# The delta rule's doubling levels with 64 moving columns instead of 128, stale columns cleared by GpSimd, the loop over levels unrolled

## The reference

```python
def chunked_gated_delta_rule(q, k, v, g, beta):
    G = jnp.cumsum(g, axis=-1)
    decay = jnp.where(lower_incl, jnp.exp(jnp.where(lower_incl, diff, 0.0)), 0.0)
    m = jnp.where(strict, jnp.einsum('bhncd,bhnsd->bhncs', kb, k) * decay, 0.0)
    a_mat = eye + m
    t_mat = lax.linalg.triangular_solve(a_mat, eye, left_side=True, lower=True)
    u = jnp.einsum('bhncs,bhnse->bhnce', t_mat, vb)
    w = jnp.einsum('bhncs,bhnsd->bhncd', t_mat, kb * jnp.exp(G)[..., None])
    attn = jnp.einsum('bhncd,bhnsd->bhncs', q, k) * decay
    # then, chunk by chunk:
    v_new = u_n - w_n @ state
    o_n = qg_n @ state + attn_n @ v_new
    state = state * exp(gl_n) + k_dec.T @ v_new
```

## Time and profile before

| | us |
|---|---|
| median of 3 executions | 2548.59 (2548.0 to 2549.6) |
| the profiled execution, its own time | 2549.39 |
| its span, first to last instruction | 2547.5 |
| its mean granted clock | 0.939 |

### The profile page before, as it was taken

The page is one execution under the profiler, slowest core; times in us unless marked ns, Lnnn a source line. Parts: engine busy times, 40 slices in busy tenths (PEclk is TensorE's granted clock), DMA queues, the critical chain, the costliest instruction groups (busy, mean ns, idle before and its releaser), DMA issues.

```text
span 2547.5 us, 32468 instructions
## 1 busy us (share of the span) xinstructions
PE 2315.7 (91%) x11904; PEld 1958.9 (77%) x11904; DVE 1683.0 (66%) x2158; ACT 1157.6 (45%) x1664; POOL 354.2 (14%) x141
## 2 busy tenths in 40 slices
PE   8998998899989989989989899899797847999999
PEld 6887887778868878878887688688687836887877
DVE  5765665478667757756654687677566643667997
ACT  4444453364444434444533644444352013546875
POOL 3531000000025315410000000244001010000000
PEclk9998999889989989999988899899899956999999
DMA  8765543234657657656432345576340000657996
GB/s 299 237 211 150 166 133 104 88 124 136 195 184 237 214 164 237 226 153 175 132 109 86 113 145 181 174 238 225 108 140 10 0 1 6 208 189 252 358 361 235
DMA packets 320162, 426.91 MB, mean 168 GB/s; under 512 B 28192, under 2 KB 220080, under 8 KB 319904
## 3 DMA queue, kind: packets, MB, share of 16 engines
q1 hardware_dynamic: 315904, 412.45, 50.7%
q0 software_dynamic: 4016, 12.73, 1.7%
q10 hardware_dynamic: 112, 0.04, 0.0%
HBM read 424.06 MB, written 1.05 MB: 167 GB/s over the span
## 4 chain that ended last, share of the span: by engine, by line
PE 74%; DVE 8%; issue 8%; ACT 6%; DVEq 2%; DMA 1%; POOL 1%; PEld 1%; POOLq 0%; SPq 0%; ACTq 0%; PEldq 0%
PE ps L264 17%; PE ps L266 17%; PE ps L265 17%; PE ps L511 10%; PE ps L3167 4%; ACT hi L247 3%; DVE lo L251 2%; PE ps L297 2%; PE ps L1053 1%; ACT room L929 1%; DVE room L1138 1%; PE ps L502 1%; DMA raw<-in_w_up 1%; DVEq L1095 1%; DVEq L730 1%
## 5 line engine op out<-in xcount | busy, mean ns | idle before, releaser
L251 DVE TENSOR_TENSOR lo<-raw,hi 128x1024 fp32r<-128x1024 f32 x737 | 1012.6, 1389 | 618.3 <-ACT hi L247 612.2
L247 ACT CAST hi<-raw 128x1024 fp32r<-128x1024 f32 x737 | 769.1, 1048 | 867.9 <-PE ps L266 695.9
L264 PE MATMUL ps<-hi,xT_hi 128*128 128x512 f32 (+2 forms) x1440 | 575.9, 400 | 5.7 <-issue 5.0
L266 PE MATMUL ps<-hi,xT_lo 128*128 128x512 f32 (+2 forms) x1440 | 563.2, 391 | 0.0
L265 PE MATMUL ps<-lo,xT_hi 128*128 128x512 f32 (+2 forms) x1440 | 563.1, 391 | 0.0
L264 PEld LDWEIGHTS ps<-hi,xT_hi 128*128 128x128 f32 x1440 | 280.5, 195 | 58.7 <-issue 6.5
L266 PEld LDWEIGHTS ps<-hi,xT_lo 128*128 128x128 f32 x1440 | 279.7, 194 | 57.2
L265 PEld LDWEIGHTS ps<-lo,xT_hi 128*128 128x128 f32 x1440 | 280.6, 195 | 51.4
L681 POOL TENSOR_SCALAR room<-room,vecs 128x1536 f32<-128x1536 f32 x28 | 134.9, 4819 | 235.8 <-DMA room<-in_w_ada 235.8
L264 PE MATMUL ps<-xT_hi,hi 128*128 128x256 f32 x544 | 160.9, 296 | 0.0
L265 PE MATMUL ps<-xT_lo,hi 128*128 128x256 f32 x544 | 155.4, 286 | 0.0
(11 more groups left out here) (526 smaller groups left out, 3348.6 us busy)
## 6 DMA issues: line engine op xcount, KB each, us to landing
raw<-in_w_mix_in SPq DMA_DIRECT2D x368, 256.0 KB, 2.9
raw<-in_ffn_w_in SPq DMA_DIRECT2D x352, 256.0 KB, 3.4
raw<-in_ffn_w_out SPq DMA_DIRECT2D x176, 256.0 KB, 2.9
raw<-in_w_gate SPq DMA_DIRECT2D x128, 256.0 KB, 5.1
raw<-in_w_up SPq DMA_DIRECT2D x128, 256.0 KB, 6.6
raw<-in_w_down SPq DMA_DIRECT2D x128, 256.0 KB, 5.7
room<-in_w_ada SPq DMA_DIRECT2D x32, 768.0 KB, 6.4
raw<-in_w_branch SPq DMA_DIRECT2D x96, 256.0 KB, 3.0
```

Source lines behind the costliest of these rows:

```text
L247: nc.scalar.copy(hi[c.hi_slot][:, 0:c.cols], raw[c.slot][:, 0:c.cols]).then_inc(rounded, 1)
L251: nc.vector.tensor_tensor(lo[c.slot][:, 0:c.cols], raw[c.slot][:, 0:c.cols], hi[c.hi_slot][:, 0:c.cols], ALU.subtract).then_inc(split, 1)
L264: pe.matmul(out, a[0], b[0], start=start, stop=False)
L266: return pe.matmul(out, a[1], b[0], start=False, stop=stop)
```

## The change

Level v changes only every second block of 2^v columns of `T` and of `Tt`, 64 of 128 columns. The changed kernel multiplies only these. For `T` TensorE multiplies `mT` itself, not masked, with the even blocks of `T`, and VectorE masks the 64 resulting columns as it takes them out of PSUM into the even blocks of `U`. Then `Tt` times the even blocks of `U` changes `T`, and `U` times the odd blocks of `Tt` changes `Tt`. `U` as a whole is the stationary operand of the second, so its odd blocks, which hold values of earlier levels, are set to zero by GpSimd between levels. GpSimd also fills `T` and `Tt` with the identity and `U` with zero at the start. The triangle goes into the subtraction by a table of 0 and -1e30. ScalarE has no part in the levels. The loops are unrolled, the tail's semaphores are merged, and `carry(pe)` is dropped.

```diff
+        ("upto_least", np.where(p <= j, 0, NEG)),
-        parts.append((f"level{b}", ((j // b) % 2 == 1) & (p // b == j // b - 1)))
+        parts.append((f"level{b}", p // b == c // b * 2 + 1))
...
+        U_BANK, T_BANK, TT_BANK = (2, 4), (3, 5), (0, 6)
...
+        def blocks(self, ap, v, odd):
+            return ap.rearrange("p (n two b) -> p n two b", two=2, b=1 << v)[:, :, odd, :]
+        def of_slot(self, ap, s):
+            return ap[:, s * P:(s + 1) * P]
+        def product(self, bank, v):
+            return ps[:, bank, :].rearrange("p (n b) -> p n b", b=1 << v)
...
+            for e in range(2):
+                nc.gpsimd.tensor_copy(self.T[e].rearrange("p (s n) -> p s n", n=P), eye)
+            pool.wait_ge(self.split, self.SPLIT_QG)
+            for e in range(2):
+                nc.gpsimd.memset(self.U[e], 0.0)
+            for e in range(2):
+                ins = nc.gpsimd.tensor_copy(self.Tt[e].rearrange("p (s n) -> p s n", n=P), eye)
+            ins.then_inc(self.cleared, 1)
+            for v in range(LEVELS - 1):
+                for e in range(2):
+                    if v == 0:
+                        pool.wait_ge(self.level, e + 1)
+                    pool.wait_ge(self.upd_t, 2 * v + e + 1)
+                    nc.gpsimd.memset(self.blocks(self.U[e], v + 1, 1), 0.0).then_inc(self.cleared, 1)
...
-            carry(pe)
...
+            for v in range(LEVELS):
+                for e in range(2):
+                    if v == 0:
+                        pe.wait_ge(self.mats, self.MT + e + 1)
+                    else:
+                        pe.wait_ge(self.level, 2 * (v - 1) + e + 1)
+                    for s in range(8):
+                        t = self.of_slot(self.T[e], s) if v else ident
+                        ins = pe.matmul(ps[:, self.U_BANK[e], s * HD2:(s + 1) * HD2], self.mT[e][:, s, :], self.blocks(t, v, 0), start=True, stop=True)
+                    ins.then_inc(self.lt, 1)
                 for e in range(2):
...
+                    pe.wait_ge(self.masked, 2 * v + e + 1)
+                    if v:
+                        pe.wait_ge(self.level_t, 2 * (v - 1) + e + 1)
+                    else:
+                        pe.wait_ge(self.mats, self.AT + e + 1)
+                    if 0 < v < LEVELS - 1:
+                        for s in range(8):
+                            ins = pe.matmul(ps[:, self.T_BANK[e], s * HD2:(s + 1) * HD2], self.of_slot(self.Tt[e], s), self.blocks(self.of_slot(self.U[e], s), v, 0),
+                                            start=True, stop=True)
+                        ins.then_inc(self.upd, 1)
+                    if v:
+                        pe.wait_ge(self.cleared, self.START + 2 * (v - 1) + e + 1)
+                    for s in range(8):
+                        t = self.of_slot(self.Tt[e], s) if v else ident
+                        ins = pe.matmul(ps[:, self.TT_BANK[e], s * HD2:(s + 1) * HD2], self.of_slot(self.U[e], s), self.blocks(t, v, 1), start=True, stop=True)
+                    ins.then_inc(self.upd_t, 1)
...
-                    nc.scalar.copy(self.LT[e][:, 0:4, :], view_bank(4 * e, 4, P)).then_inc(self.lt0_done, 1)
...
-                V.tensor_tensor(self.e[e], self.e[e], bc(const("upto").unsqueeze(1), [P, 8, P]), ALU.mult)
+                V.tensor_tensor(self.mT[e], self.e[e], big(self.KK_BANK[e]), ALU.mult).then_inc(self.mats, 1)
+            for v in range(LEVELS):
+                at, b = CONSTS[f"level{1 << v}"][0], 1 << v
+                mask = consts[:, at:at + P // 2].rearrange("p (n b) -> p n b", b=b)
+                if v == 0:
+                    dve.wait_ge(self.cleared, self.START)
+                for e in range(2):
+                    dve.wait_ge(self.lt, 2 * v + e + 1)
+                    u = self.U[e].rearrange("p (s n two b) -> p s n two b", s=8, two=2, b=b)[:, :, :, 0, :]
+                    V.tensor_tensor(u, ps[:, self.U_BANK[e], :].rearrange("p (s n b) -> p s n b", s=8, b=b),
+                                    bc(mask.unsqueeze(1), [P, 8, P // 2 // b, b]), ALU.mult).then_inc(self.masked, 1)
+                    if v == 0:
+                        dve.drain()
+                        t = self.blocks(self.T[e], 0, 0)
+                        V.tensor_tensor(t, t, self.blocks(self.U[e], 0, 0), ALU.subtract).then_inc(self.level, 1)
+                if v == 0:
+                    dve.wait_ge(self.gram, self.QK)
+                    for e in range(2):
+                        V.tensor_tensor(self.aT[e], self.e[e], big(self.QK_BANK[e]), ALU.mult).then_inc(self.mats, 1)
+                for e in range(2):
+                    if 0 < v < LEVELS - 1:
+                        dve.wait_ge(self.upd, 2 * (v - 1) + e + 1)
+                        t = self.blocks(self.T[e], v, 0)
+                        V.tensor_tensor(t, t, self.product(self.T_BANK[e], v), ALU.subtract).then_inc(self.level, 1)
+                    dve.wait_ge(self.upd_t, 2 * v + e + 1)
+                    t = self.blocks(self.Tt[e], v, 1)
+                    V.tensor_tensor(t, t, self.product(self.TT_BANK[e], v), ALU.subtract).then_inc(self.level_t, 1)
                 dve.drain()
```

More of the change, by code:

```diff
@@ L2103, in build @@
         SPREAD0, SPREAD1, KK, QK = 1, 2, 3, 4
[L2104 to L2108, removed]
+        SPREAD_BANK, KK_BANK, QK_BANK = (0, 6), (2, 4), (0, 6)
+        level, level_t, upd, upd_t = sem("g_level"), sem("g_level_t"), sem("g_upd"), sem("g_upd_t")
+        mats, lt, masked, cleared = sem("g_mats"), sem("g_lt"), sem("g_masked"), sem("g_cleared")
+        MT, AT, START = 0, 2, 1
+        U_BANK, T_BANK, TT_BANK = (2, 4), (3, 5), (0, 6)
+        tail, tail_done, wT_done = sem("g_tail"), sem("g_tail_done"), sem("g_wT_done")
+        U0, STATE, VNEW, OUT = 1, 3, 5, 7
         raw = room[0:CT * CONV, 14000:14000 + P]
@@ L2119, in build @@
         e, mT, aT = ([view(room, 6144 + 2048 * n + 1024 * e, 8, P) for e in range(2)] for n in range(3))
[L2120 to L2123, removed]
+        U = [room[:, 12288 + 1024 * e:12288 + 1024 * (e + 1)] for e in range(2)]
+        T = [merged[:, e, :] for e in range(2)]
+        Tt = [xT_work[:, D * e:D * (e + 1)] for e in range(2)]
         vn = [view(hi_ring, 3072 + 512 * e, 8, HD2) for e in range(2)]
@@ L2213, in pe @@
             self.pe_gram(pe, self.QK_BANK, self.qT)
-            heads = self.heads
-            carry(pe)
[L2217 to L2229, removed]
@@ L2248, in pe @@
             cols = lambda h: slice(h * HD2, (h + 1) * HD2)
             for e in range(2):
-                pe.wait_ge(self.level, LEVELS * 2 + e + 1)
+                pe.wait_ge(self.level_t, 2 * (LEVELS - 1) + e + 1)
                 for h in range(4):
-                    pe.matmul(ps[:, 4 * e, cols(h)], self.Tt[e][:, h, :], self.head(self.vb, 0, e, h), start=True, stop=True)
-                    ins = pe.matmul(ps[:, 4 * e + 1, h * P:(h + 1) * P], self.both(self.kg, 1, h), self.Tt[e][:, 4 + h, :], start=True, stop=True)
@@ L2254, in pe @@
-                ins.then_inc(self.u0, 1)
+                    pe.matmul(ps[:, 4 * e, cols(h)], self.of_slot(self.Tt[e], h), self.head(self.vb, 0, e, h), start=True, stop=True)
+                    ins = pe.matmul(ps[:, 4 * e + 1, h * P:(h + 1) * P], self.both(self.kg, 1, h), self.of_slot(self.Tt[e], 4 + h), start=True, stop=True)
+                ins.then_inc(self.tail, 1)
             for e in range(2):
-                pe.wait_ge(self.u0_done, e + 1)
+                pe.wait_ge(self.tail_done, self.U0 + e)
@@ L2439, in dve @@
-            for e in range(2):
-                dve.wait_ge(self.lt, LEVELS * 2 + e - 1)
-                copy_lt(e)
-            for e in range(2):
-                dve.wait_ge(self.upd, LEVELS * 2 + e - 3)
-                V.tensor_tensor(self.Tt[e], self.Tt[e], big(4 * e), ALU.subtract)
-                dve.drain()
-                dve.sem_inc(self.level, 1)
-            for e in range(2):
-                dve.wait_ge(self.u0, e + 1)
-                V.tensor_copy(self.vn[e][:, 0:4, :], ps[:, 4 * e, 0:256].rearrange("p (h n) -> p h n", n=HD2)).then_inc(self.u0_done, 1)
```

81 lines of the change are left out of this document (19 added, 62 removed).

## The result

The changed kernel takes 2599.75 us (median, 2595.71 to 2600.88) against 2548.64 before: 1.0197 times, with an interval of 1.018 to 1.0215. The forecast was 2597. Its profiled execution took 2600.43 us, with a span of 2598.7 and a mean granted clock of 0.916 (0.939 before).

The account below looks back on a forecast made before the run. The level was taken as bound by its matmul count, with a short VectorE chain between. With the clock lost in level 0, +42.8 us to the tail and slower tail matmuls made +48.8, so 2597 us, range 2585 to 2609.

Parts of the forecast that it names:

- The bound and the price: Delta-rule levels: bound by matmul count; a 64-column matmul costs what 128 does, 0.223 us at 2.4 GHz, 0.427 at 1.2.
- The fall of the clock: Level 0, after its first products: TensorE waits 2.7 us for aT, the clock falls and stays down through all levels.
- 64-column matmuls neither hold nor win back 2.4 GHz.: Read from the delta rule's trace, 2032 to 2036 and 2108 to 2118 us: narrow matmuls stay at clock 0.50.
- Rival (A): Level 0's pause: the clock holds through the 2.7 us, matmuls cost 0.223 us, kernel takes 2533 us; chance 7%.
- Rival (B): Levels: the clock falls and comes back as TensorE runs without a gap, kernel takes 2536 us; chance 3%.
- The sum: Whole kernel: +42.8 us up to the tail's start and slower tail matmuls, in all +48.8, giving 2597 us.
- the +0.3: Start of the delta rule: subtractions as scalar_tensor_tensor cost 0 to 1.2 us more, taken as +0.3.
- The term for GpSimd beside VectorE: Angle computations after 1931 us: GpSimd's clearing beside them may cost 0 to 2 us; taken as 0, +2 kept.
- +6.0: The tail: its first 7 us run at 1.2 instead of 2.4 GHz, adding 3.3, 1.5 and 1.2 us.
- No wait on `g_cleared`: Levels: GpSimd's memset has over 10 us before TensorE's wait for it, so it costs nothing.
- (C): Levels: columns set the matmul price, half the columns cost half, kernel takes 2509 us; chance 1%.
- (D): First two levels: gapped columns or operand switches make 64 matmuls cost 0.617 instead of 0.427 us, 2609 us; chance 5%.

Follow-up runs that it names:

- experiment 6: Changed kernel, level 0's second product written to free banks so it need not wait, GpSimd's clearing moved behind the first subtractions: 2527.43 us; with clearing unmoved 2537.64 us.
- Experiment 8: Kernel without level 0's pause, clearing moved, with a short pause before level 3: one added clearing 2567.65 us, two 2568.40; one with 128 moving columns 2533.71.
- experiment 3: Changed kernel with 14 added unused matmuls of 128 moving columns filling level 0's pause: 2541.09 us.
- experiment 4: Changed kernel with 14 added unused matmuls of 64 moving columns filling level 0's pause: 2541.57 us, one of nine executions 2602.63.
- experiment 2: Changed kernel with only the first product of each level streaming its 64 moving columns twice, as 128: 2544.54 us.
- experiment 7: Kernel without level 0's pause, clearing moved, six added clearings making TensorE pause before level 3: 2576.69 us; with 128 columns and level 0's pause kept: 2542.33.
- experiment 5: Changed kernel with GpSimd's clearing of U and filling of Tt moved behind VectorE's first subtractions: 2597.26 us.
- experiment 1: Changed kernel with the levels' matmuls streaming their 64 moving columns twice, as 128: 2539.09 us.

## Why the prediction was right, point by point

**The bound and the price.** Right. The level is bound by the number of matmuls, and 64 columns cost what 128 do. At 1.2 GHz a level takes 20.48 us, 48 x 0.427. At 2.4 GHz it takes (2000.29 - 1946.70) / 5 = 10.72 in experiment 6, 48 x 0.223. That the weight loads of 128 columns set this price is argued from PEld, busy 96.00 of 96 us; no run changed the stationary columns.

**The fall of the clock.** Right in place and in consequence, with one part of the reasoning off. I put the pause (2.7 forecast, 2.79 measured) between one of 1.68 us that did no harm and one of 3.80 that did, as if its length decided. Experiment 8 shows that length is not the measure among 64-column matmuls: 1.37 us are enough. What I had put beside it, the 64-column work, is what decides: the run that differs only in having 128 columns kept its clock through the same 1.37 us. Whether the columns ahead of the pause or those behind it count was not separated.

**"64-column matmuls neither hold nor win back 2.4 GHz."** Half of that was wrong. They hold it, for 64 to 68 us in the kernels of experiments 3, 4 and 6. The rows I read it from, 2032 to 2036, are of the tail, where small pauses and matmuls over 64 rows are mixed in. The forecast rested on the other half, and that is true of the gap-free streams inside the levels, not everywhere: behind the QK gram (128 columns, at 1.2 GHz for 3.79 us) the clock came back 1.1 to 1.4 us into 64-column matmuls, in the changed kernel and in the same place in experiments 4 and 6 (there in the run with the clearing unmoved). In experiment 3, where it had fallen only inside the gram, it did not. What decides between these was not tested. Had the clock come back in the same way behind the pause of level 0, the forecast would have failed; it did in none of the executions of the changed kernel (2595.71 to 2600.88). Rival (A) is what happens as soon as the pause is gone: I gave it 2533, and the kernel without the pause, with the clearing where the change has it, takes 2537.64.

**Rival (B)**, that gap-free work brings the clock back, was cited from the Trainium skill, "TensorE: Matmul & The Clock Gate", section "Why this matters for your kernels". The runs bear it out for 128 columns (experiments 2, 3, 7) and, inside the levels, not for 64: 96.00 busy of 96 us at 0.50.

**The sum** came out right in part by luck, with errors that cancel: predicted was +48.8, the spans of the profiled executions differ by 51.2. Predicted from the start to the tail was +42.8, measured is 2073.86 - 2027.75 = +46.1 (the tail's first matmul, L2272, starts at 2073.86). The subtractions took 4.22 us as before, so the +0.3 was nothing. The term for GpSimd beside VectorE, taken as 0 with +2 kept for the range, was 2.1. The gram at 1.2 GHz (3.79 for 2.06 us, +1.7) and a slower first product (4.39 for the 3.79 of experiment 6, +0.6) were not in the sum; they follow from the 3.88 us wait, which the same GpSimd work had lengthened. The fall came somewhat after the pause, which gave 0.8 back (6.21 for 7.03 us). With the 2.79 us pause that is 2.1 - 0.3 + 1.7 + 0.6 - 0.8 + 0.1 = 3.4, the difference but for 0.1. In the tail I had +6.0; from its start to VectorE's last copy in it (2089.06) it took 15.2 us against 14.3 (2027.75 to 2042.08), +0.9: its first matmuls, of which every second has 128 columns, ran at 0.50 for 5 us, and then the clock was back, 0.99 from 2079 to 2086. The remaining +4.2 of the span lies behind the delta rule, in code that did not change. One place where it arises is a stretch 140 us behind VectorE's first instruction of the norm (2056.25 before, 2103.22 after). Before, it reads

```profile
2196.25:2216.25 20.00, 20.00 (x103) 16.88 (x102) 12.25 (x16) 8.38 (x14) 0.00 (x0) 1.00 0.72 240
```

and in the changed kernel

```profile
2243.22:2263.22 20.00, 20.00 (x95) 16.72 (x94) 12.42 (x15) 9.14 (x14) 0.00 (x0) 0.91 0.72 230
```

There too the clock differs. From the norm's reduction on VectorE to the end the profiles of all kernels show 489.6 to 496.4 us, with 491.4 and 496.0 for the two kernels of experiment 8 that differ by one clearing. So this part moves from one execution to the next, and no cause was looked for.

**The rest.** No wait on `g_cleared`, twelve memsets of 0.52 to 0.59 us hidden, VectorE never late in a level: as predicted. Rivals (C) and (D) did not show: level 1, with blocks of 2, takes the same 20.48 us as the others.

## What to carry to other kernels

Halving the moving columns of a matmul whose stationary side stays 128 wide saved no time here, and behind a gap in the narrow stream the clock did not come back. Without a gap the stream ran at full clock for 64 to 68 us, and one gap of 1.4 us cost all that followed: so before narrowing matmuls, find each wait that is left in the stream, and remove it (another bank, another order on the engine waited for) in the same edit. Where the wait must stay, two things helped here: added matmuls without use in its place (experiments 3 and 4), and one 128-column product behind it (experiment 2).

## What the hardware showed that I had not expected

- The clock has two steady courses for one and the same gap-free stream of 64-column fp32 matmuls: 0.50 for 96 us in the changed kernel, 1.00 for 64 to 68 us in experiments 3, 4 and 6. Only what came ahead of the stream differs.
- It can fall after the pause and not in it: after 1.37 us of pause it was at 1.00 for 2 us more of full work, then 0.62, then 0.50. After level 0's 2.79 us it fell about 1 us after the pause in the changed kernel, and in experiment 5 within it.
- Streaming 128 columns instead of 64 costs nothing at 2.4 GHz (a level takes 10.7 to 10.9 us in experiment 1 and 10.7 in experiment 6), and kept the clock through the same 1.37 us.
- A cast of two columns on VectorE took six times as long, 0.93 us for 0.16, beside a GpSimd memset on SBUF, and ended with it; subtractions that read PSUM beside such a memset took the same 4.22 us.
